# Norms computed inside the feed-forward stages, rope angles on VectorE, and centred values in the delta rule of a three-block transformer kernel

## The reference

```python
hn = rms_norm_2(h, attn_norm[l])
proj = hn @ w_in[l]
# the delta rule, per token and head, state of 64 x 64:
sa = einsum('bhvk,bhk->bhv', state, -kkt)
state = state * wt + sa * (kkt * at) + vt * kt
y = einsum('bhvk,bhk->bhv', state, rt)
mean = jnp.mean(y, axis=-1, keepdims=True)
var = jnp.mean(jnp.square(y - mean), axis=-1, keepdims=True)
# y is normalized by mean and var, scaled, gated; y_b is retention, y_c latent attention
mix = concatenate([y_a, y_b, y_c], axis=-1)
h = h + mix @ w_out[l]
hn = rms_norm_2(h, ffn_norm[l])
gu = hn @ w_gate_up[l]
h = h + (silu(gu[..., :D_FF]) * gu[..., D_FF:]) @ w_down[l]
```

## Time and profile before

| | |
|---|---|
| median of 3 runs | 3696.68 us (3691.38, 3696.68, 3696.89) |
| the profiled execution | 3690.88 us |
| its span from first to last instruction | 3689.0 us |
| PE, DVE, ACT, POOL busy | 87%, 39%, 30%, 8% of the span |
| granted TensorE clock, mean | 0.939 of full speed |

### The profile page before, as it was taken

How to read it: one execution, slowest core, us unless ns; L and a number is a source line. 1 busy time by engine, 2 the same in 40 slices (tenths; PEclk the granted TensorE clock), 3 DMA queues, 4 the chain that set the end, 5 groups by cost and what they waited for, 6 DMA issues and landing times. The chain is left out here.

```text
span 3689.0 us, 42190 instructions
## 1 busy us (share of the span) xinstructions
PE 3225.8 (87%) x16302; PEld 2284.4 (62%) x16302; DVE 1442.2 (39%) x2412; ACT 1118.4 (30%) x1905; POOL 301.8 (8%) x289
## 2 busy tenths in 40 slices
PE   7999999998687887887774988799998998879997
PEld 5777888877333333333333857678886856868886
DVE  5772666643410000000004566443323467443322
ACT  4673677742000000000003343232222344232221
POOL 1000222200000000000000002200000001300000
PEclk9999999999799999999996998899999998989999
DMA  5222222223899999999984200023323300023332
GB/s 111 64 68 71 81 69 69 69 75 101 337 426 426 426 426 424 423 420 411 419 341 140 69 12 4 24 85 93 101 97 81 87 12 4 1 92 97 92 102 75
DMA packets 355575, 601.99 MB, mean 163 GB/s; under 512 B 72336, under 2 KB 306608, under 8 KB 330672
## 3 DMA queue, kind: packets, MB, share of 16 engines
q1 hardware_dynamic: 346160, 590.85, 43.8%
q0 software_dynamic: 9216, 8.42, 0.7%
HBM read 603.40 MB, written 20.97 MB: 169 GB/s over the span
## 5 line engine op out<-in xcount | busy, mean ns | idle before, releaser
L1800 PE MATMUL ex_up<-ex_W,ex_XT 128*64 128x512 f32 x1024 | 259.9, 666 | 89.5 <-DMA ex_W<-in_w_expert_up_dram 89.5
L226 ACT ACTIVATE f_hi<-f_raw 128x1024 fp32r<-128x1024 f32 x148 | 156.8, 1059 | 564.7 <-PE ff_bk L286 547.7
L1800 PE MATMUL ex_gp<-ex_W,ex_XT 128*64 128x512 f32 x1024 | 243.5, 630 | 59.5 <-DMA ex_W<-in_w_expert_gate_dram 58.1
L235 DVE TENSOR_TENSOR f_lo<-f_raw,f_hi 128x1024 fp32r<-128x1024 f32 x148 | 181.1, 1224 | 256.4 <-ACT f_hi L226 256.2
L284 PE MATMUL ff_bk<-h_a_hi,f_hi 128*128 128x512 f32 x704 | 275.6, 392 | 2.8 <-DVE h_a_lo L3555 2.8
L285 PE MATMUL ff_bk<-h_a_lo,f_hi 128*128 128x512 f32 x704 | 275.2, 391 | 0.0
L286 PE MATMUL ff_bk<-h_a_hi,f_lo 128*128 128x512 f32 x704 | 274.9, 390 | 0.0
L1829 PE MATMUL ex_yp<-ex_W,ex_hT 128*64 128x512 f32 x1024 | 228.5, 598 | 37.1 <-DMA ex_W<-in_w_expert_down_dram 22.3
L1843 DVE TENSOR_TENSOR ex_hid<-ex_sg,ex_up 128x512 f32<-128x512 f32 x32 | 22.0, 688 | 610.8 <-PE ex_up L1800 610.8
L1800 PEld LDWEIGHTS ex_up<-ex_W,ex_XT 128*64 128x64 f32 x1024 | 93.0, 152 | 256.0 <-issue 256.0
L1800 PEld LDWEIGHTS ex_gp<-ex_W,ex_XT 128*64 128x64 f32 x1024 | 88.3, 144 | 213.8 <-issue 212.0
(11 more groups left out here) (618 smaller groups left out, 6615.1 us busy)
## 6 DMA issues: line engine op xcount, KB each, us to landing
ex_W<-in_w_expert_gate_dram SPq DMA_DIRECT2D x64, 2048.0 KB, 28.8
ex_W<-in_w_expert_up_dram SPq DMA_DIRECT2D x64, 2048.0 KB, 28.9
ex_W<-in_w_expert_down_dram SPq DMA_DIRECT2D x64, 2048.0 KB, 29.0
b_raw<-in_w_in_dram SPq DMA_DIRECT2D x88, 512.0 KB, 3.8
f_raw<-in_w_gate_up_dram SPq DMA_DIRECT2D x88, 512.0 KB, 3.9
f_raw<-in_w_down_dram SPq DMA_DIRECT2D x44, 512.0 KB, 3.6
m_raw<-in_w_in_dram SPq DMA_DIRECT2D x40, 512.0 KB, 3.9
b_raw<-in_w_branch_ssd_dram SPq DMA_DIRECT2D x16, 512.0 KB, 4.1
```

Of the source, the lines that this page charges most:

```text
L226: a.activation(self.hi[n % self.SLOTS][:, at], self.raw[n % self.RAW][:, at], ACT.Copy).then_inc(self.cast, 1)
L235: v.tensor_tensor(self.lo[i][:, at], self.raw[n % self.RAW][:, at], self.hi[i][:, at].bitcast(F32), ALU.subtract).then_inc(self.split_done, 1)
L1800: ins = pe.matmul(ps[part[e], :], XT[b][:, q, part[e]], row_view(slots[e], KD)[:, q, :], start=(q == 0), stop=(q == KD - 1))
```

## The change

- `stage_start`: GpSimd does `rope.phases` only. The positions are loaded behind all tiles of x instead of ahead of the last two. VectorE reduces both halves of the angles in `stage_attention`, by the three-operand instruction.
- `stage_mix`: two more units get side work, `centred0` (unit 21) and `centred1` (unit 23). Each is four matmuls of values by a 128x128 matrix (identity minus one 64th within a head, built by GpSimd), copied by ScalarE into `vc`. `vc` lies in the space of the retention tile. `vt` stays as it was.
- `stage_delta`: all products with values use `vc`, so that the mean of each head's `y` is zero. The mean and the difference are gone, and the square has moved to ScalarE. The order of the end on VectorE and ScalarE is new.
- `stage_ffn`: the last three down tiles of the second half (`TAIL` = 3) are held together and multiplied token tile by token tile. Each finished token tile is added, squared, normed and scaled while TensorE works on the next. With layer 0 the result is transposed between the matmuls (`turn_next`) and split into `h_hi`, `h_lo`, which both layers now share; the first three weight tiles of layer 1 are loaded before the stage ends. With layer 1 each token tile is stored by a DMA of its own.
- `stage_norm` and `stage_store` are gone.

```diff
@@ stage_ffn, SyncE @@
                 W.load_until(sp, len(W.tiles))
+                sp.wait_ge(f_lo, BLOCKS)
+                sp.dma_start(next_row[:], row_bc(next_w)).then_inc(row_loaded, 16)
+                if following is not None:
+                    sp.wait_ge(W.used, DOWN + DR + 5)
+                    following.load_until(sp, following.RAW)
+                else:
+                    for t in range(NT):
+                        sp.wait_ge(last_ready, t + 1)
+                        sp.dma_start(out_rows[t], k.x[:, t, :]).then_inc(stored, 16)
+                    sp.wait_ge(stored, 16 * NT)
@@ stage_ffn, TensorE @@
+                for t in range(NT):
+                    for r in range(DR - TAIL, DR):
+                        if t == 0:
+                            W.wait(pe, DOWN + DR + r)
+                        for q in range(2):
+                            ins = mm3(pe, bk[4 + t][:], both(fT, 2 * r + q, slice(t * P, (t + 1) * P)), W.tile(DOWN + DR + r, q), False, r == DR - 1 and q == 1)
+                    ins.then_inc(acc_ready, 1)
+                    if following is not None and t >= 1:
+                        turn_next(t - 1)
+                if following is not None:
+                    turn_next(NT - 1)
@@ stage_ffn, ScalarE @@
+                for t in range(NT):
+                    last_square(1, t)
+                    last_root_of(t)
+                    if following is not None and t >= 1:
+                        next_hi(2 * t - 2)
+                        next_hi(2 * t - 1)
@@ stage_ffn, VectorE @@
+                for t in range(NT):
+                    last_add(t)
+                    if following is not None and t >= 2:
+                        next_lo(2 * t - 4)
+                    last_mean_of(t)
+                    if following is not None and t >= 2:
+                        next_lo(2 * t - 3)
+                    last_scale(t)
+                if following is not None:
+                    for g in range(2 * NT - 4, 2 * NT):
+                        next_lo(g)
@@ stage_delta, VectorE @@
                 def spread(t):
-                    v.drain()
-                    do(v.tensor_reduce, mean[:, t, :], heads(y, t), AX, ALU.add)
-                    do(v.tensor_scalar, mean[:, t, :], mean[:, t, :], 1.0 / 64, None, ALU.mult)
-                    do(v.tensor_tensor, heads(y, t), heads(y, t), each(mean, t), ALU.subtract)
-                    do(v.tensor_tensor, sq[:, t, :], y[:, t, :], y[:, t, :], ALU.mult)
+                    v.wait_ge(squared, t + 1)
                     do(v.tensor_reduce, var[:, t, :], heads(sq, t), AX, ALU.add)
@@ stage_mix, TensorE @@
+                def centre_v(half):
+                    bank = x_bank(f"centred{half}")
+                    pe.wait_ge(v_done, 1)
+                    pe.wait_ge(centre_ready, 1)
+                    for t in range(2):
+                        for b in range(2):
+                            ins = pe.matmul(bank[:, t * RW + b * P:t * RW + (b + 1) * P], rkv[:, 4 + b, tok(2 * half + t)], centre, start=True, stop=True)
@@ stage_start, GpSimd @@
                 rope.phases(g)
-                rope.reduce(g, (0,))
@@ stage_attention, VectorE @@
-                rope.reduce(v, (1,))
+                rope.reduce(v, (0, 1))
```

More of the change, by code:

```diff
@@ L188, with __init__ @@
     RAW = SLOTS = 3
-    def __init__(self, k, ctx, tag, tiles):
-        self.tiles, self.issued = tiles, 0
-        self.raw = [k.sb(f"{tag}_raw{i}", [P, 1024], F32, ctx) for i in range(self.RAW)]
-        self.hi = [k.sb(f"{tag}_hi{i}", [P, 1024], F32R, ctx) for i in range(self.SLOTS)]
-        self.lo = [k.sb(f"{tag}_lo{i}", [P, 1024], F32R, ctx) for i in range(self.SLOTS)]
+    def __init__(self, k, ctx, tag, tiles, early=None):
+        self.tiles, self.issued, self.tag, self.early = tiles, 0, tag, early
+        if early is None:
+            self.settle(k, ctx)
+        else:
+            self.raw = [k.over(f"{tag}_early{i}", [P, 1024], F32, early + 4096 * i) for i in range(self.RAW)]
         lasting = lambda n: k.nc.alloc_semaphore(name=f"{tag}_{n}")
@@ L197, in __init__, with settle @@
         self.cast, self.split_done, self.used = lasting("w_cast"), lasting("w_split_done"), lasting("w_used")
+    def settle(self, k, ctx):
+        assert self.early is None or k.next_left() == self.early
+        raw = [k.sb(f"{self.tag}_raw{i}", [P, 1024], F32, ctx) for i in range(self.RAW)]
+        if self.early is None:
+            self.raw = raw
+        self.hi = [k.sb(f"{self.tag}_hi{i}", [P, 1024], F32R, ctx) for i in range(self.SLOTS)]
+        self.lo = [k.sb(f"{self.tag}_lo{i}", [P, 1024], F32R, ctx) for i in range(self.SLOTS)]
     def close(self, k):
@@ L295, with __init__ @@
 class RopeTable:
-    def __init__(self, k, ctx, tag, positions, freq, cos_out, sin_out, apart=False):
+    def __init__(self, k, ctx, tag, positions, freq, cos_out, sin_out):
         self.k, self.positions, self.freq, self.cos, self.sin = k, positions, freq, cos_out, sin_out
@@ L2529, in stage_mix @@
 @stage
-def stage_mix(k, layer, M, at, rkv, krT, latT, w_kv_up, cos32, sin32, v_first, out, eb, vt, gt, bonus, ret, mix):
+def stage_mix(k, layer, M, at, rkv, krT, latT, w_kv_up, cos32, sin32, v_first, out, eb, vt, vc, gt, bonus, ret, mix):
     nc = k.nc
@@ L2782, in extras @@
                         decay(2)
+                    if name in ("centred0", "centred1"):
+                        bank, free = from_x(name)
+                        half = int(name[7])
+                        a.activation(vc[:, 2 * half:2 * half + 2, :].rearrange("p t n -> p (t n)"), bank[:], ACT.Copy).then_inc(free, 1)
                     if u == 25:
@@ L2977, in stage_delta @@
 @stage
-def stage_delta(k, l, out, eb, vt, gt, bonus, spent, at, gn_w, gn_b, mix):
+def stage_delta(k, l, out, eb, vt, vc, gt, bonus, spent, at, gn_w, gn_b, mix):
     nc = k.nc
@@ L3233, in _ @@
                     take_parts(t)
-                for t in range(NT):
-                    root(t)
+                square(0)
+                square(1)
+                root(0)
+                square(2)
+                root(1)
+                square(3)
+                root(2)
+                root(3)
             @block.vector
@@ L3328, in _ @@
                 spread(1)
+                normalize(0)
+                add_outputs(3)
                 spread(2)
                 normalize(1)
-                add_outputs(3)
                 spread(3)
@@ L3385, in stage_ffn @@
 @stage
-def stage_ffn(k, l, W, base, mix, norm_w):
+def stage_ffn(k, l, W, base, mix, norm_w, next_w, following, out_rows):
     nc = k.nc
@@ L3409, in stage_ffn @@
         sig_ready, f_ready, f_hi, f_lo = sem("sig_ready"), sem("f_ready"), sem("f_hi"), sem("f_lo")
+        row_loaded, last_squared, last_mean, last_root, last_ready, last_turned, last_hi, last_lo, stored = (sem("last_" + n) for n in (
+            "row", "squared", "mean", "root", "ready", "turned", "hi", "lo", "stored"))
         h = (k.h_hi, k.h_lo)
+        TAIL = 3
         part = lambda x, g: x[:, (g % 2) * 4:(g % 2) * 4 + 4, (g // 2) * P:(g // 2 + 1) * P]
@@ L3618, in first_block @@
                 k.make_room_for_rope("1", att_ctx)
-                rope = RopeTable(k, att_ctx, "r1", ap["positions"], "freq64", k.cos, k.sin, apart=True)
+                rope = RopeTable(k, att_ctx, "r1", ap["positions"], "freq64", k.cos, k.sin)
                 stage_start(k, W, ap["x"], ap["norm_mix_w"][0], rope)
```

208 lines of the change are left out of this document (101 added, 107 removed).

## The result

The changed kernel takes 3655.33 us, median of 4 runs (3645.15 to 3656.36), beside 3694.03 for the kernel before on the same chip (4 runs, 3687.18 to 3696.89). The ratio is 0.9896, 95% interval 0.9884 to 0.9908: 34 to 43 us faster. The profiled execution took 3656.36, its span is 3654.5 and the mean granted clock 0.941, against 3690.88, 3689.0 and 0.939.

What follows compares the result with a forecast made beforehand. TensorE mostly paces inside stages; at the boundaries the last engine to finish sets the time. Terms 6.4 + 11.4 - 1.0 + 7.8 + 13.1 = 37.7 us, taken from 3693.8, gave 3656 us; 3648 to 3669 holds 8 in 10 or more.

Steps and rivals of the forecast that it cites:

- the likeliest case: Whole kernel: the sum of all terms comes as laid out, own range 3650 to 3664 us, chance 0.75.
- Angles, +6.4: Start stage and attention's first tiles: GpSimd's reduction moved to VectorE, 6.28 + 0.6 - 0.5 = 6.4 us gained (4 to 7).
- The 0.5 of waiting: Attention's start: the reduction on VectorE delays `make_lo(2)`, so TensorE waits 0.5 us for that tile.
- Delta rule, +11.4: End of the delta rule: VectorE's stretch falls from 18.9 to 13.2 us per layer, 11.4 gained in two (8 to 13.8).
- Centred values, -1.0: Latent attention: added matmuls and ScalarE copies cost 0.5 us per layer, 1.0 lost in both (0 to 6).
- End of layer 0, +7.8: Layer 0 to layer 1: norm hidden behind held-back matmuls, layer 1 starts at E + 10.95 against E + 18.75, 7.8 us gained (5 to 9).
- E: Feed-forward stage: the time its matmuls would end if no transposes stood between them, 2821.2 in the profile before.
- End of the program, +13.1: Program end: last tile scaled at 3671.6, its 512 KB store lands in 3.5 us, 13.1 us gained (11.5 to 14).
- half the gain: Rival: delta rule, centring and layer 0's end fall short, only 22 us gained, 3672 or 3669 us, chance 0.12.
- the stores don't queue: Denies a rival at program end: four stores of 6.6 us each queue, gain 2.5 instead of 13.1, 3667 us, chance 0.04.
- the angles pay: Denies a rival in attention: VectorE's 4.3 us delay later tiles, 4 of 6.9 us come back as waits, 3660, chance 0.06.
- no feed-forward stage stayed at 1.2 GHz: Denies the slower rival: TensorE at 1.2 GHz in a feed-forward stage, 0.227 us more per matmul, 3708 us, chance 0.03.

Runs made afterwards that it cites:

- second measurement: The changed kernel unaltered, timed again beside the kernel before: 3650.29 us (5 runs), 0.9902 of before.
- the first pair: First profiles of the kernel before and the changed kernel: spans 3689.0 and 3654.5 us, profiled executions 3690.88 and 3656.36 us.

## Why the prediction was right, and where its terms were not

The forecast was 3656 us, the median 3655.3, and the likeliest case came: each stage end moved because the engine that ended it last lost work or had it hidden. That the number came within 1 us is luck in part, since the second measurement of the same kernel has 3650.3, and at the places the terms were 2.6 us too small in sum. The terms:

- **Angles, +6.4.** The barrier gave 6.22 of 6.28. The 0.6 for x issued sooner was nothing: the last two tiles were issued 0.7 us sooner, but VectorE's last low part ended at 23.76 against 23.67, so it had not been waiting for x's issue. The 0.5 of waiting was nothing either: the low part came at 37.52, just in time. Two mistakes of one size and opposite sign, so the sum stood, by luck.
- **Delta rule, +11.4.** 12.3 in the first pair, 12.8 by means over all profiles (19.15 before, 12.76 changed, per layer). The length laid out, 13.2, was 13.0 and 12.9. What I did not see is that the order of the queue was no part of the gain, and a small loss in it.
- **Centred values, -1.0.** The one copy whose place was read cost 0.43, in layer 0; ScalarE's rows in layer 1 fall behind by the same 0.4. -0.9.
- **End of layer 0, +7.8.** 8.5. The wait ahead of the first transposes was 0.7, not 0.5, TensorE was done at E + 2.7 for the 2.6 laid out, VectorE at E + 9.4 for 10.2. Two sums don't come out as written: the durations of tile 0's chain make 4.50 and not 4.59, and those behind TensorE's end make E + 7.3 for the last scaling and not E + 6.8. It was E + 6.7, since the low parts fill VectorE's waits for ScalarE and don't come on top of the chain. The four last low parts were sized by a chain that ran alternately with ScalarE; here half of them were ready and ran back to back (x2 in the row).
- **End of the program, +13.1.** 13.8. The last scaling ended 3.8 us after E as laid out; the store landed in 2.6 us, and 3.5 had been taken from a load.

In sum 40.3 at the places against 37.7, and 38.7 and 38.4 between the medians of the two measurements. The 2 us between places and medians have no place of their own; the clock's steps and the first 100 us of layer 0's feed-forward stage, told above, are larger than that. **The rivals:** half the gain is out by every place; the stores don't queue (2.6 us each, issued 3.6 to 4.0 us apart); the angles pay; and no feed-forward stage stayed at 1.2 GHz. TensorE was granted that level for 20 to 30 us of it up to E with three held-back tiles, for 26 and 27 in the kernel before.

The clock did act elsewhere, and it is what the prediction had no term for. The delta rule up to its end has taken one of three lengths in 28 stretches of 14 profiles: 108.0 to 108.7 us (13 times), 112.3 to 112.6 (11) or 116.3 to 116.9 (4), with 8 to 9, 18 to 19 and 32 to 34 us of it at 1.2 GHz. All of that lies at the start of the stage: TensorE is at the low level when the stage begins, and what differs is how long it stays there. Two such stages with steps of 4.1 us can make up a good part of the 10 to 15 us by which executions of one kernel differ here. So two profiles are not compared by their spans. Why TensorE is given one length or another is open: no run set out to steer it.

## What to carry to other kernels

Read a stage's end by the engine that ends it, count the instructions that leave that engine, and then check each reordering by itself: here sixteen instructions fewer gave the whole gain and the new order took 0.5 us back. To hide a norm behind matmuls, hold back as many weight tiles as make one token tile's matmuls (4.08 us) longer than its chain (3.64 us); with one tile 14 of 22 us of the gain were lost. Compare two kernels place by place when an execution carries steps of 4 us that belong to neither.

## What the runs showed of the hardware that was not expected

- The delta rule's small matmuls take 108, 112 or 116 us by how long TensorE stays at 1.2 GHz from the stage's start (8, 18 or 33 us), in the same kernel from one execution to the next.
- VectorE's TENSOR_TENSOR of 128x256 took 0.42 us alone and 0.79 to 0.97 in layer 1 beside GpSimd, whose own took 0.72; moving six of them saved 1.1 us, not 2.3.
- Stores landed in 2.0 us (256 KB), 2.6 (512 KB) and 6.6 (2048 KB), the loads of 512 KB here in 3.3 to 4.4.
- A table load of 1.28 us, ahead of the first mean of the tail, cost 0.9 us at the end of layer 0 and nothing at the end of the program; a square root on a spare value moved it into ScalarE's idle time.
